# Two transformer stacks on one core: a ring of 3 raw and 3 split weight tiles instead of 2 and 4, and a gate activation one place earlier

## The reference

```python
for layer in range(4):
    x = x + 0.5 * swiglu(rms_norm(x, ffn1_norm[layer]), ffn1_w_gu[layer], ffn1_w_down[layer])
    x = x + mixer(rms_norm(x, mix_norm[layer]))      # hgrn2, neighbourhood, latent, hgrn2
    x = x + 0.5 * swiglu(rms_norm(x, ffn2_norm[layer]), ffn2_w_gu[layer], ffn2_w_down[layer])
# swiglu(x) = (silu(x @ w_gate) * (x @ w_up)) @ w_down, inner width 2816

x = layer_norm(ALPHA * x + rg_lru(x));            x = layer_norm(ALPHA * x + conv_ffn(x))
x = layer_norm(ALPHA * x + stick_breaking(x));    x = layer_norm(ALPHA * x + conv_ffn(x))
# conv_ffn(x): h = causal_conv3(x @ w_up); (gelu(h[:, :3072]) * h[:, 3072:]) @ w_down
```

## Time and profile before

| | us |
|---|---|
| median of 3 runs | 3272.21 (3271.46 to 3274.34) |
| the profiled execution's own time | 3273.65 |
| its span, first to last instruction | 3271.8 |
| TensorE busy | 2948.0, 90% of the span |
| VectorE busy | 2020.8, 62% |
| ScalarE busy | 1367.7, 42% |
| mean granted TensorE clock | 0.953 of full speed |

### The profile page before, as it was taken

One profiled execution on the slowest core, in us unless ns is written; L12 is line 12 of the kernel. 1 busy time (PEld: TensorE's weight loads), 2 busy tenths in 40 slices (PEclk: granted clock), 3 DMA queues, 4 the chain that ended last, 5 costly groups with the idle time before them and its releaser, 6 DMA issues.

```text
span 3271.8 us, 44866 instructions
## 1 busy us (share of the span) xinstructions
PE 2948.0 (90%) x19567; PEld 2679.1 (82%) x19567; DVE 2020.8 (62%) x2245; ACT 1367.7 (42%) x1430; POOL 313.7 (10%) x391
## 2 busy tenths in 40 slices
PE   6997779999988999999899999786999798796987
PEld 6997769999976999985499999786899698694986
DVE  5557775555657656543655555777556666747666
ACT  4444434444444444433544344443444433343433
POOL 0005430000002000000000000544000100000000
PEclk9998989999989999999899999898999799897998
DMA  5543325565531655532146455332454444441443
GB/s 188 192 156 106 98 80 168 193 193 196 165 129 39 206 193 168 193 107 82 52 156 204 152 199 178 116 101 80 153 195 142 159 151 155 141 159 61 160 170 108
DMA packets 362056, 478.12 MB, mean 146 GB/s; under 512 B 9226, under 2 KB 324324, under 8 KB 361860
## 3 DMA queue, kind: packets, MB, share of 16 engines
q1 hardware_dynamic: 358448, 467.30, 43.0%
q0 software_dynamic: 1776, 6.77, 0.7%
q10 hardware_dynamic: 1636, 1.18, 0.1%
HBM read 474.17 MB, written 1.05 MB: 145 GB/s over the span
## 4 chain that ended last, share of the span: by engine, by line
PE 65%; DVE 20%; ACT 7%; DMA 5%; issue 3%; ACTq 0%; SPq 0%; DVEq 0%
PE Wk L547 12%; PE Wk L548 12%; PE Wk L549 12%; PE Y L547 7%; PE Y L548 7%; PE Y L549 7%; DVE w_lo L1470 6%; ACT w_hi L1061 4%; DMA ring<-in_ffn_w_up 3%; DVE work L1693 2%; PE Wk L555 1%; DVE work L1603 1%; DVE work L1599 1%; DVE work L1696 1%; PE Y L857 1%
## 5 line engine op out<-in xcount | busy, mean ns | idle before, releaser
L1470 DVE TENSOR_TENSOR w_lo<-ring,w_hi 128x2048 fp32r<-128x2048 f32 x436 | 1002.4, 2306 | 757.3 <-ACT w_hi L1061 717.1
L547 PE MATMUL Wk<-xT_hi,w_hi 128*128 128x256 f32 x4320 | 1235.5, 286 | 33.4 <-DVE xT_lo L1502 18.4
L548 PE MATMUL Wk<-xT_lo,w_hi 128*128 128x256 f32 x4320 | 1228.1, 284 | 0.0
L549 PE MATMUL Wk<-xT_hi,w_lo 128*128 128x256 f32 x4320 | 1227.7, 284 | 0.0
L1061 ACT ACTIVATE w_hi<-ring 128x2048 fp32r<-128x2048 f32 x436 | 828.7, 1907 | 693.1 <-DMA ring<-in_ffn_w_gu 257.7
L547 PEld LDWEIGHTS Wk<-xT_hi,w_hi 128*128 128x128 f32 x4320 | 835.3, 193 | 43.1 <-issue 23.3
L548 PEld LDWEIGHTS Wk<-xT_lo,w_hi 128*128 128x128 f32 x4320 | 835.1, 193 | 4.6 <-issue 0.9
L549 PEld LDWEIGHTS Wk<-xT_hi,w_lo 128*128 128x128 f32 x4320 | 834.6, 193 | 0.0
L547 PE MATMUL Y<-w_hi,hid_hi 128*128 128x512 f32 x896 | 358.6, 400 | 48.7 <-DVE w_lo L1470 31.6
L548 PE MATMUL Y<-w_lo,hid_hi 128*128 128x512 f32 x896 | 354.3, 395 | 0.0
L549 PE MATMUL Y<-w_hi,hid_lo 128*128 128x512 f32 x896 | 353.2, 394 | 0.0
(11 more groups left out here) (250 smaller groups left out, 3046.4 us busy)
## 6 DMA issues: line engine op xcount, KB each, us to landing
ring<-in_ffn_w_gu SPq DMA_DIRECT2D x176, 1024.0 KB, 5.1
ring<-in_ffn_w_down SPq DMA_DIRECT2D x112, 1024.0 KB, 5.0
ring<-in_ffn_w_up SPq DMA_DIRECT2D x48, 1024.0 KB, 5.2
ring<-in_hg_w_in SPq DMA_DIRECT2D x40, 1024.0 KB, 5.1
ring<-in_na_w_in SPq DMA_DIRECT2D x12, 1024.0 KB, 5.2
ring<-in_hg_w_out SPq DMA_DIRECT2D x8, 1024.0 KB, 4.9
ring<-in_lru_w_in SPq DMA_DIRECT2D x8, 1024.0 KB, 5.5
ring<-in_kv_w SPq DMA_DIRECT2D x8, 1024.0 KB, 5.5
```

What stands on the lines that cost most here:

```text
L547: pe.matmul(o, l_hi, r_hi, start=first, stop=False)
L548: pe.matmul(o, l_hi, r_lo, start=False, stop=False)
L549: return pe.matmul(o, l_lo, r_hi, start=False, stop=last)
L1470: dve.tensor_tensor(lo, raw(t), hi.bitcast(F32), ALU.subtract).then_inc(lo_done, 1)
```

## The change

The ring of raw tiles grows from two to three, the ring of split tiles shrinks from four to three, and in the ScalarE order of a feed-forward chunk the gate step comes ahead of the high copy of the next up tile. Nothing else changes: the loads, the products and the order on the other engines are the same.

```diff
-RAW, SPLIT = 2, 4
+RAW, SPLIT = 3, 3
...
                     splits(g + 3)
                     if j == 0 and has_norm(s):
                         save_r(s)
+                    gate(j, j % 2, g)
                     splits(g + 4)
-                    gate(j, j % 2, g)
                     rest(j, j % 2, g)
```

## The result

| | before | after |
|---|---|---|
| median | 3273.28 us (3271.46 to 3275.60, 4 runs) | 3367.82 us (3366.61 to 3368.12, 4 runs) |
| span of the profiled execution | 3271.8 | 3366.3 |
| mean granted clock | 0.953 | 0.94 |

The ratio after to before is 1.0288, 95% interval 1.027 to 1.0306. The forecast was 3362 us in 3320 to 3392, with 0.93 on slower: direction, size and mechanism came out. Its losses came out 15.1 us too small and its gains 10.5 us too small, and these two misses nearly cancelled: that the value is within 6 us is in part luck.

A forecast was written before the change was run, and what follows sets the result against it. What counts was whether a weight or hidden half comes later than TensorE asks. Losses 109.5, less gains 53.5, plus 34 of clock gave +90 us: 3362 us, range 3320 to 3392.

The forecast's parts named there:

- The two stands: Eight plain feed-forward ends: TensorE waits 4.3 and 4.9 us after T (end of last up product), plus 0.25; 75.6 us.
- The clock: Half clock behind 18 new stands at plain feed-forward and attention ends, 1.9 us each; 34 us lost.
- the hg ends: Ends of the two gated recurrent mixers: output product 4.1 us later, residual add 1.1 more; 10.4 us lost.
- The attention ends: Ends of neighbourhood and latent attention: the same tile pair without a hidden half, 5.1 us each; 10.2 us lost.
- The cffn chunks: Convolution feed-forward, eleven chunks twice: third raw buffer ends DMA waits, 17.0 us a chunk; 28.2 us gained.
- the two cffn ends: Tails of the two convolution feed-forwards: last hidden half comes earlier; 7.5 and 4.7 us gained.
- Ways in: Seven ways into a feed-forward stage: row copy delayed behind the fourth tile's copy, net 0.6 us each; 4.5 us lost.
- The middle of a stage: Inside plain feed-forward stages: nothing changes, 17.0 us a chunk, hidden half with 7 to 10 us to spare.
- The clock holds: Rival: no half clock behind the new stands; 3328 us, chance 0.14.
- Stage ends are cheap: Rival: third-buffer gains land and the eight feed-forward ends cost below 2.4 us each; 3219 at no cost, chance 0.04.
- The middle gives way: Rival: slow loads reach TensorE inside stages, 1 us in each of 80 chunks; 3440 us, chance 0.05.
- The third raw buffer brings nothing: Rival: double buffering already suffices, so no gains from the third raw buffer; 3416 us, chance 0.03.

The follow-up runs named there:

- fill: The changed kernel with useless products into an unused PSUM bank in both stands of the eight plain feed-forward ends; 3335.52 us.
- both_first: The changed kernel with the next sublayer's first tile split behind the last hidden half, its second behind residual add or first half of norm statistics; 3232.77 us.
- all_first: both_first, plus hg's last step not splitting the next sublayer's first tile, and the row copy ahead of the fourth tile's copy on ways in; 3203.23 us.
- order_r2s4: all_first with the rings of the kernel before (2 raw, 4 split) and the gate step in its old place; 3271.28 us.
- add_first: The changed kernel with only the next sublayer's second tile split later, behind the residual add or first half of norm statistics; 3287.29 us.

## Why the prediction was right, by its steps

**The two stands: right, and 0.6 us an end too short.** It said 4.3 us, ended by the hidden low part at T+7.0, and 4.9 us, ended by the residual add. The trace has 4.35 and 4.99 us with those releasers. The second tile's copy was to start at T+12.5 without the clock; with it, it starts at 226.33, T+15.1. The experiments take each stand away by itself, with the products, the copies and the rings unchanged, so the mechanism is shown and not only argued. The waiting that `fill` leaves is 80.6 us, where the prediction had 75.6. The idle time in the two rows isn't all of it, since running products overlap: by the starts of TensorE's instructions, measured from T, the product behind the first stand comes 4.5 us later than before, and the transposes a further 5.1, and 0.25 more went to the second transposes, as forecast.

**The clock: right in size, too narrow in place.** 1.9 us for each of 16 stands in plain ends; `fill` gives 1.95. But the sum left the hg ends out, and this is its largest miss: 8.6 us. Its shift of the output product was right (the stand before it is 0.82 us before and 4.95 us after, 4.1 as forecast), and the eight products behind it then ran at 0.50, 3.78 us for 1.99. TensorE's row before:

```profile
2289.15 1.99 PE L778 MATMUL Wk<-work 128*128 128x256 f32 x8 [0.82 <-DVE work L1683]
```

That is a 19th and a 20th stand. Half clock lasts 9.6 us behind it (the 2411.56:2421.14 row above), longer than behind any of the 18; the term was 10.4 for both ends and measured 19.0. That part is read from the trace and not tried by itself; `both_first`, which leaves that step alone, keeps 8.4 us at each hg end, and `all_first`, which changes it (and a step at the ways in, elsewhere), has 31.42 us from there to the next sublayer's second tile, as before. The attention ends were 14.5 for 14.0.

**The cffn chunks: right in kind, mis-sized by the count.** It said 17.0 us a chunk and used 11 x 17.0 = 187. From the end of one up tile to the eleventh after it there are 22 gate and up tiles of 5.76 us but only 10 down tiles of 5.46, since the first chunk has none ahead of its next up product: 181.3. The trace has 181.7, and 181.3 without the moved gate step. For two stages the slip is 11.4 us; 10.6 were missing in the term (28.2 forecast, 38.8 measured). Its 14.8 us of VectorE's load in a chunk was too high as well: the trace has 138.5 us in eleven, 12.6 each. At the two cffn ends the hidden half came at T+11.6 and T+7.6, nearly as laid out (11.5 and 7.4), but the gains came out 1.4 and 1.2 us smaller than forecast.

**Small terms.** Ways in +4.8 for 4.5; stick -4.9 for 4.6; latent attention -6.2 for 4.2 (I have not traced the other 2 us); lru's end 3.7 and stick's 4.8 for 4.4 each.

**The middle of a stage: right.** 166.00 us over ten chunks of the third sublayer at clock 1.00, 164.6 in `all_first`: the difference is the stand on the way in, nothing inside.

**How +90 met +94.5.** Losses were forecast at 143.5 (109.5 and 34 of clock) and measured 158.6: 8.6 of the miss are the hg ends, 5.8 the plain feed-forward ends (5.0 of waiting, 0.8 of clock). Gains were forecast at 53.5 and measured 64.0, nearly all of that miss in the cffn chunks. Two misses of 15.1 and 10.5 us with opposite signs leave 4.6.

**The rivals.** "The clock holds" (3328) fell: all 18 stands have half clock behind them, for 2.9 to 6.2 us. "Stage ends are cheap" (3219) fell with this order, but its number is close to what `both_first` reaches (3233), by the way it named: the next sublayer's tiles copied elsewhere than ahead of the last multiply and the residual add. "The middle gives way" fell at 166.00. "The third raw buffer brings nothing" (3416), the rival by the Trainium skill ("Trainium Kernel Development and Optimization", Best Practices) that one double-buffers to overlap DMA with compute: this case disagrees for a loop in which copy, low part and load follow each other. Two raw buffers gave 204.2 to 211.1 us in the first cffn in the four kernels that have them, three gave 181.3 to 181.7.

## What to carry to other kernels

A buffer count is a statement on how far a queue may run ahead, so before lowering it list what stands behind the copy that will be held, on its engine and on the engine that follows it: here two tiles that nobody needed for 10 us held up a 0.7 us step and an add that TensorE was waiting for, and moving them cost no time and was worth 135 us. Price both resources of such a trade and the order at once: depth of loads without the order lost 94 us, order without the depth gave nothing, and the two together gained 70. When a term is "n chunks of t", count the instructions between the two marks, for the first and last chunk are seldom whole.

## What the runs showed of the hardware

**The price of a stand of four to five microseconds doesn't end with it.** At the 18 stands of the plain feed-forward and attention ends the clock fell to 0.50 in the stand, in four of them up to 0.7 us after it, and stayed there for about 3 to 6 us of work; behind the two hg stands it stayed for 9.6 us. Keeping TensorE busy with useless products through the same waits took 31.2 us off 16 stands. Not every stand is followed by half clock: behind the two of 2.17 us at the cffn ends of `all_first` the granted clock is 1.00 through the whole last down tile.

**A weight load issued beside two loads of the same size from GpSimd's queue took three times as long.** In `order_r2s4` the load of the way-in tile was issued at 683.84, 1.9 and 1.0 us behind GpSimd's two loads of a table, 1000 KB each. The DMA issues of that stretch (KB each, median us to landing):

```profile
ring<-in_ffn_w_gu SPq DMA_DIRECT2D x1, 1024.0 KB, 15.0
```

By the page of the changed kernel it is 4.9 to 5.5 us for the large groups of weight loads. The traces of `add_first`, `both_first` and `all_first` show it too: the one weight load issued at the same distance behind the table's took 14.8, 14.6 and 15.3 us. In the other seven traces, those of the kernels before and after among them, no weight load is issued while the first of the table's two is under way. With three raw buffers the late load costs little: that stage of `all_first` is 1.0 us longer than its like. Whether the 6 us come in every execution of `order_r2s4` I have not tested.
